# The experts' 512-column weight blocks laid out even columns first, and read by every product a column of either half in turn

## The chip, the cores and the metric

The kernel runs on one core of one Trainium2 chip. The metric is device time in microseconds, of the slowest (here the only) core. Before the change it is 1811.17 us, the median of three runs (1811.16 to 1812.86).

## The reference

A decoder trunk of two layers for 272 token rows (256 tokens and 16 learned meta rows), width 1024. Each layer is a token mixer (two linear-attention branches with their projections), a layer norm, a channel mixer and a second layer norm. The channel mixer of layer 0 is a dense SwiGLU; that of layer 1 is a top-2-of-8 expert SwiGLU with a hidden width of 3584. It is the experts that the change touches:

```
def swiglu(x, w_gate, w_up, w_down):
    return (jax.nn.silu(x @ w_gate) * (x @ w_up)) @ w_down

def moe_swiglu(x, w_router, w_gate, w_up, w_down):
    ...
    out = jnp.zeros(t.shape, jnp.float32)
    for e in range(N_EXPERTS):
        out = out + combine[:, e:e + 1] * swiglu(t, w_gate[e], w_up[e], w_down[e]).astype(jnp.float32)
```

All weights are float32: 8 x (1024 x 3584) for gate and for up, 8 x (3584 x 1024) for down, 352 MB in all.

## The kernel before

**Weights as units.** The host reorders the weights so that one load brings a unit: 128 partitions x 2048 float32 (1 MB), `UNIT`. SyncE loads the units in the order in which they are used into `raw`, a ring of six. ScalarE writes a rounded copy (`w_hi`, type float32r, a ring of three), VectorE writes the remainder raw - w_hi (`w_lo`, also float32r, a ring of three). A product of two float32 matrices is then three TensorE products, low x high, high x low, high x high (`mm3`, lines 796 to 800), accumulated in PSUM in float32.

**The experts' stage.** The tokens of an expert (up to 128) are gathered into `xg_hi`, `xg_lo`, transposed, so that they are the stationary operand (128 x 128); the weights are the moving operand, 512 columns at a time (`COLS`). An expert has seven chunks (`JCH`) of 512 hidden columns. A chunk is six units: two for gate, two for up (in each four blocks of 128 rows x 512 columns, `gate_or_up`, line 1153), two for down (in each two blocks of 128 rows x 1024 columns, read as two halves of 512, `down`, line 1186). That is 16 block products for gate and up and 8 for down, each of three matmuls: 72 matmuls of 512 columns in a chunk. Beside them stand four transposes of the gated hidden values (`turn_piece`, line 1176). Eight experts give 56 chunks. `expert` (from line 1233) orders them; on TensorE it is one straight line of work, with a wait on `lo_ready` before each unit (`expert_unit`, line 1149) and a signal `units_used` behind each.

**Who waits for whom.** ScalarE's rounding of a unit waits for the load of the unit and for `units_used` of the unit three before it. VectorE's remainder waits for ScalarE's `hi_ready` (`lo`, line 1999). SyncE's load into a slot of `raw` waits for `lo_ready` of the unit six before it. Between them VectorE also multiplies gate by up (line 2330) and makes the remainder of the turned hidden values (line 2320), ScalarE takes silu and rounds the hidden values.

**The rest of the kernel** (both token mixers, the dense SwiGLU, norms, router) has the weights as the stationary operand (128 x 128) and the tokens as the moving one, 272 or 256 columns (`feature_major`). Some of its products are in plain float32: attention (`inside`, line 999, whose moving operand is read in pieces of 32 columns, and `across`, line 1003, whose moving operand is one run of 256), the score products and the router.

Of the kernel before, what the change touches and what calls it, by code (L numbers as in the profile page):

```python
# [28 lines left out]
P = 128  # L29
D = 1024  # L30
# [10 lines left out]
EXPERTS = 8  # L41
# [4 lines left out]
COLS = 512  # L46
ROW = 320
RAW, HALVES = 6, 3
JCH = DFFE // COLS
# [58 lines left out]
def dense_units():  # L108

    stream = []  # L110

    def add_cols(src, c0, cols=COLS):
        for k in range(0, KT, 4):
            stream.append(("cols", src, k, 4, c0, cols))

    for l in range(DEPTH):
        w_in = ("w_in", l)
        def pair(src, c0):
            add_cols(src, c0)
            add_cols(src, c0 + COLS)  # L120

        if l == 0:
            stream.extend(("cols", w_in, k, 1, COL["gk"], COLS) for k in range(4))
            stream.extend(("cols", w_in, k, 2, COL["gk"], COLS) for k in (4, 6))
        else:
            add_cols(w_in, COL["gk"])
        add_cols(w_in, COL["gq"])
        stream.append(("twice", w_in, 0, KT, COL["ga"], P))
        pair(w_in, COL["gv"])
        add_cols(w_in, COL["gate_a"])  # L130
        add_cols(w_in, COL["gate_a"] + COLS)
        add_cols(w_in, COL["gate_b"])
        pair(w_in, COL["gr"])
        add_cols(w_in, COL["rq"])
        add_cols(w_in, COL["rk"])
        pair(w_in, COL["rv"])
        pair(("w_pa", l), 0)
        pair(w_in, COL["rg"])
        add_cols(w_in, COL["gate_b"] + COLS)
        pair(("w_pb", l), 0)  # L140
        pair(("w_o", l), 0)
        if l == 0:
            for c0 in range(0, DFF, COLS):
                n = min(COLS, DFF - c0)
                add_cols(("ffn_w_gate", 0), c0, n)
                add_cols(("ffn_w_up", 0), c0, n)
            for c in range(2):
                for k in range(0, DFF // P, 4):
                    stream.append(("cols", ("ffn_w_down", 0), k, min(4, DFF // P - k), c * COLS, COLS))
    return stream  # L150


def unit_major(a, rows):

    *lead, r, c = a.shape
    a = a.reshape(*lead, r // rows, rows // P, P, c).swapaxes(-3, -2)
    return a.reshape(*lead, r // rows, P, rows // P * c)


def weight_units(inputs):  # L160

    stream = dense_units()
    dense = np.zeros((len(stream), P, UNIT), np.float32)
    for u, (kind, (name, i), k, kn, c0, n) in enumerate(stream):
        cols = np.arange(c0, c0 + n) if kind == "cols" else c0 + np.arange(n) % RANK
        dense[u, :, 0:kn * n] = unit_major(np.asarray(inputs[name])[i][k * P:(k + kn) * P, cols], kn * P)[0]
    units = dict(dense_units=dense, moe_w_down=unit_major(np.asarray(inputs["moe_w_down"][0]), 2 * P))
    for name in ("moe_w_gate", "moe_w_up"):
        a = np.asarray(inputs[name][0]).reshape(EXPERTS, D, JCH, COLS).swapaxes(1, 2)
        units[name] = unit_major(a, 4 * P)  # L170
    return units

# [23 lines left out]
def trunk(nc, w, consts, where, out):  # L196

    ctx = ExitStack()
    with ctx:
# [43 lines left out]
        def quadrant(h, rows=BLOCK):  # L243
            return slice(h * BLOCK, h * BLOCK + rows)
# [299 lines left out]

        plan_sets()
        number = {(l, name): r for r, (l, name, _, _) in enumerate(sets)}
        ends = [u for _, _, u, _ in sets]
        NSETS = len(sets)

# [110 lines left out]
        block = ctx.enter_context(nc.Block())  # L660
# [131 lines left out]
        def _(pe):  # L792
            used = 0

            def mm3(dst, l_hi, l_lo, r_hi, r_lo, start, stop):


                nc.tensor.matmul(dst, l_lo, r_hi, start=start, stop=False)  # L798
                nc.tensor.matmul(dst, l_hi, r_lo, start=False, stop=False)  # L799
                return nc.tensor.matmul(dst, l_hi, r_hi, start=False, stop=stop)  # L800
# [85 lines left out]
            def repeated(columns, times):  # L886
                return columns.unsqueeze(1).broadcast_to([P, times, columns.shape[1]])
# [140 lines left out]
            for l in range(DEPTH):  # L1028
# [12 lines left out]
                for h in range(HEADS):  # L1041
                    last = nc.tensor.matmul(pt[:, h, 0:T], a2[quadrant(h), l, :], gaT[quadrant(h), :], start=True, stop=True)
# [79 lines left out]
            for t in range(2):  # L1122
                last = nc.tensor.transpose(pt[:, 2, (t + 1) * P:(t + 2) * P], mean_and_std[:, t, :], ident)
# [16 lines left out]
            last = nc.tensor.matmul(pt[0:1, 2, 0:P], ones[:, 0:1], repeated(sel[:, 1, :], P // EXPERTS), start=False, stop=True)  # L1140
# [5 lines left out]
            Y = ps[1][:, 0:2, :]  # L1146
            X = ps[1][:, 2:4, :]

            def expert_unit(at, u):
                pe.wait_ge(lo_ready, u + 1)  # L1150
                return w_hi[:, at % HALVES, :], w_lo[:, at % HALVES, :]

            def gate_or_up(dst, at, u, o, gathers_of=None, woven=None):
                for i in range(2):
                    if woven is not None and i == 1:
                        turn_may(woven)
                    if gathers_of is not None:
                        pe.wait_ge(gather_hi_ready, START + 4 * gathers_of + 2 * o + i + 1)
                        pe.wait_ge(gather_lo_ready, START + 4 * gathers_of + 2 * o + i + 1)
                    u_hi, u_lo = expert_unit(at + i, u + i)  # L1160
                    for k in range(4):
                        if woven is not None and i == 1:
                            turned = turn_piece(k)
                            if k == 3:
                                turned.then_inc(hidden_turned, 1)
                        last = mm3(dst, xg_hi[:, o, 4 * i + k, :], xg_lo[:, o, 4 * i + k, :],
                                   u_hi[:, k * COLS:(k + 1) * COLS], u_lo[:, k * COLS:(k + 1) * COLS],
                                   start=(i == 0 and k == 0), stop=(i == 1 and k == 3))
                    last.then_inc(units_used, 1)

            def turn_may(k):

                pe.wait_ge(hidden_ready, START + k + 1)
                pe.wait_ge(hidden_lo_ready, START + k)

            def turn_piece(i):
                return nc.tensor.transpose(TB[:, i * P:(i + 1) * P], a_sl[:, i * P:(i + 1) * P], ident)  # L1177

            def turn(k):

                turn_may(k)
                for i in range(4):
                    last = turn_piece(i)
                last.then_inc(hidden_turned, 1)

            def down(at, u, k, first, final, by_half=False, hidden=None, turns=False):
                a_hi, a_lo = hidden or (ag_hi, ag_lo)
                pe.wait_ge(hidden_lo_ready, START + k + 1)
                for i in range(2):
                    if i and turns:  # L1190
                        turn(k + 1)
                    u_hi, u_lo = expert_unit(at + i, u + i)
                    halves_last = by_half and i == 1
                    for a in range(2):
                        for b in range(2):
                            kk, q = (b, a) if halves_last else (a, b)
                            o = kk * D + q * COLS
                            last = nc.tensor.matmul(Y[:, q, :], a_lo[:, 2 * i + kk, :], u_hi[:, o:o + COLS],  # L1198
                                                    start=first and i == 0 and kk == 0, stop=False)
                            nc.tensor.matmul(Y[:, q, :], a_hi[:, 2 * i + kk, :], u_lo[:, o:o + COLS], start=False, stop=False)  # L1200
                            last = nc.tensor.matmul(Y[:, q, :], a_hi[:, 2 * i + kk, :], u_hi[:, o:o + COLS],  # L1201
                                                    start=False, stop=final and i == 1 and kk == 1)
                            if halves_last and (q, kk) == (0, 1):
                                last.then_inc(half_full, 1)
                    last.then_inc(units_used, 1)
# [27 lines left out]
            def expert(m, g, e, o, seam=False, more=False, closing=False, spilled=False):  # L1233
# [22 lines left out]
                if seam:  # L1256
                    chunk(0, final=True, moved=(o == 0), entry=True)
                else:
                    pe.wait_ge(silu_ready, START + k0)
                    gate_or_up(G_, at, u0, o, gathers_of=m)  # L1260
                    pe.wait_ge(hidden_ready, START + k0)
                    gate_or_up(U_, at + 2, u0 + 2, o)
# [1244 lines left out]
```

## Time and profile before

| | |
|---|---|
| median of three runs | 1811.17 us |
| the profiled execution, its own time | 1812.49 us |
| its span, first to last instruction | 1810.8 us |
| TensorE clock granted, mean | 0.998 of full |
| TensorE busy | 1778.4 us, 98% |
| VectorE busy | 1361.4 us, 75% |
| ScalarE busy | 1112.7 us, 61% |
| HBM read | 485.85 MB |

Busy times are from a hardware profile of one execution. Matmuls are pipelined: the duration shown for one (some 390 ns for 512 columns) is longer than the distance from its start to the next one's start, so what a matmul costs is read from starts, not from durations.

### The profile page before, as it was taken

How to read it: one execution, taken by the hardware profiler on the slowest of the kernel's cores; microseconds unless marked ns; L12 is line 12 of the kernel's file. 1: busy time of each engine (PE TensorE's matmuls, PEld its weight loads, DVE VectorE, ACT ScalarE, POOL GpSimd, SP SyncE). 2: the span in 40 equal slices, each digit the busy share in tenths (PEclk: the TensorE clock that was granted, in tenths of full speed). 3: DMA queues.
4: the chain of work that ended last, by engine and by line, in shares of the span. 5: the costliest groups of instructions: out<-in, count | busy, mean ns of one | idle time of the engine just before them, and what ended most of it. 6: DMA issues, size and time to landing. Idle time of an engine off the chain costs nothing.

```text
span 1810.8 us, 28116 instructions
## 1 busy us (share of the span) xinstructions
PE 1778.4 (98%) x10872; PEld 1579.2 (87%) x10872; DVE 1361.4 (75%) x1155; ACT 1112.7 (61%) x854; POOL 77.5 (4%) x145
## 2 busy tenths in 40 slices
PE   8999999999999999999999999999999999999997
PEld 7999999999989999998887888888888888888885
DVE  4756577645466566668888888888888888888897
ACT  5544254543445442557777777777777777777775
POOL 0300200000001102000000000000000000000200
PEclk9999999999999999999999999999999999999999
DMA  8635434444535465355999989999999999999993
GB/s 337 212 125 180 165 143 161 163 163 161 195 143 186 147 208 191 114 204 202 381 365 377 377 335 387 364 381 380 350 371 366 368 386 369 350 371 369 403 419 145
DMA packets 75922, 498.63 MB, mean 275 GB/s; under 512 B 11162, under 2 KB 11674, under 8 KB 17968
## 3 DMA queue, kind: packets, MB, share of 16 engines
q1 hardware_dynamic: 68304, 482.38, 69.9%
q0 software_dynamic: 5920, 11.58, 1.9%
q10 hardware_dynamic: 1600, 3.31, 0.7%
q8 instruction: 69, 1.13, 0.2%
q14 instruction: 29, 0.24, 0.0%
HBM read 485.85 MB, written 4.72 MB: 271 GB/s over the span
## 4 chain that ended last, share of the span: by engine, by line
PE 58%; DVE 1%; issue 0%; ACT 0%; DVEq 0%; ACTq 0%
PE ps L798 13%; PE ps L800 13%; PE ps L799 13%; PE ps L1198 6%; PE ps L1200 6%; PE ps L1201 6%; PE ps L1177 1%; PE ps L1221 1%; DVE w_lo L2003 0%; PE ps L895 0%; PE ps L999 0%; PE ps L1003 0%; DVE y_out L1946 0%; DVE h_tok L2402 0%; PE ps L989 0%
## 5 line engine op out<-in xcount | busy, mean ns | idle before, releaser
L2003 DVE TENSOR_TENSOR w_lo<-raw,w_hi 128x2048 fp32r<-128x2048 f32 x335 | 764.8, 2291 | 117.1 <-ACT w_hi L1327 114.4
L1327 ACT ACTIVATE w_hi<-raw 128x2048 fp32r<-128x2048 f32 x337 | 643.7, 1912 | 189.5 <-PE ps L800 103.0
L481 DVE TENSOR_TENSOR w_lo<-raw,w_hi 128x2048 fp32r<-128x2048 f32 (+2 forms) x126 | 272.5, 2170 | 192.5 <-ACT w_hi L470 191.7
L798 PE MATMUL ps<-rows_hi,w_lo 128*128 128x272 f32 (+1 forms) x1376 | 395.6, 287 | 13.0 <-DVE w_lo L481 8.1
L800 PE MATMUL ps<-rows_hi,w_hi 128*128 128x272 f32 (+1 forms) x1376 | 393.5, 286 | 0.0
L799 PE MATMUL ps<-rows_lo,w_hi 128*128 128x272 f32 (+1 forms) x1376 | 393.4, 286 | 0.0
L798 PE MATMUL ps<-w_hi,xg_lo 128*128 128x512 f32 x896 | 369.8, 413 | 0.0
L799 PE MATMUL ps<-w_lo,xg_hi 128*128 128x512 f32 x896 | 351.6, 392 | 0.0
L800 PE MATMUL ps<-w_hi,xg_hi 128*128 128x512 f32 x896 | 351.6, 392 | 0.0
L470 ACT ACTIVATE w_hi<-raw 128x2048 fp32r<-128x2048 f32 (+2 forms) x130 | 234.3, 1807 | 177.2 <-PE ps L800 139.0
L798 PEld LDWEIGHTS ps<-rows_hi,w_lo 128*128 128x128 f32 x1376 | 260.2, 189 | 15.6 <-DVE w_lo L481 8.1
L799 PEld LDWEIGHTS ps<-rows_lo,w_hi 128*128 128x128 f32 x1376 | 260.5, 189 | 0.1
L800 PEld LDWEIGHTS ps<-rows_hi,w_hi 128*128 128x128 f32 x1376 | 260.1, 189 | 0.0
L798 PEld LDWEIGHTS ps<-w_hi,xg_lo 128*128 128x128 f32 x896 | 168.5, 188 | 47.4
L800 PEld LDWEIGHTS ps<-w_hi,xg_hi 128*128 128x128 f32 x896 | 168.3, 188 | 38.1
L799 PEld LDWEIGHTS ps<-w_lo,xg_hi 128*128 128x128 f32 x896 | 169.2, 189 | 28.0
L1198 PE MATMUL ps<-w_hi,ag_lo 128*128 128x512 f32 x440 | 172.9, 393 | 0.5 <-DVE w_lo L2003 0.5
L1200 PE MATMUL ps<-w_lo,ag_hi 128*128 128x512 f32 x440 | 172.4, 392 | 0.0
L1201 PE MATMUL ps<-w_hi,ag_hi 128*128 128x512 f32 x440 | 172.1, 391 | 0.0
L1198 PEld LDWEIGHTS ps<-w_hi,ag_lo 128*128 128x128 f32 x440 | 82.7, 188 | 19.9 <-issue 1.6
L1201 PEld LDWEIGHTS ps<-w_hi,ag_hi 128*128 128x128 f32 x440 | 82.7, 188 | 18.3
L1200 PEld LDWEIGHTS ps<-w_lo,ag_hi 128*128 128x128 f32 x440 | 82.7, 188 | 17.5
(351 smaller groups left out, 1827.0 us busy)
## 6 DMA issues: line engine op xcount, KB each, us to landing
raw<-in_dense_units SPq DMA_DIRECT2D x116, 1024.0 KB, 4.9
raw<-in_moe_w_gate SPq DMA_DIRECT2D x112, 1024.0 KB, 7.0
raw<-in_moe_w_up SPq DMA_DIRECT2D x112, 1024.0 KB, 6.8
raw<-in_moe_w_down SPq DMA_DIRECT2D x112, 1024.0 KB, 7.2
raw<-in_dense_units SPq DMA_DIRECT2D x10, 512.0 KB, 3.8
result_rows<-rows POOLq DMA_DIRECT2D x7, 512.0 KB, 8.2
v_tok<-turned_v POOLq DMA_DIRECT2D x48, 64.0 KB, 2.9
srT<-o_tok ACTq DMA_DIRECT2D x6, 272.0 KB, 4.5
```

What stands on the lines that cost most here:

```text
L470: nc.scalar.activation(w_hi[:, u % HALVES, 0:k * n], raw[:, u % RAW, 0:k * n], ACT.Copy).then_inc(hi_ready, 1)
L481: nc.vector.tensor_tensor(w_lo[:, u % HALVES, 0:k * n], raw[:, u % RAW, 0:k * n], w_hi[:, u % HALVES, 0:k * n].bitcast(F32), ALU.subtract) ...
L798: nc.tensor.matmul(dst, l_lo, r_hi, start=start, stop=False)
L799: nc.tensor.matmul(dst, l_hi, r_lo, start=False, stop=False)
L800: return nc.tensor.matmul(dst, l_hi, r_hi, start=False, stop=stop)
L1177: return nc.tensor.transpose(TB[:, i * P:(i + 1) * P], a_sl[:, i * P:(i + 1) * P], ident)
L1198: last = nc.tensor.matmul(Y[:, q, :], a_lo[:, 2 * i + kk, :], u_hi[:, o:o + COLS], start=first and i == 0 and kk == 0, stop=False)
L1200: nc.tensor.matmul(Y[:, q, :], a_hi[:, 2 * i + kk, :], u_lo[:, o:o + COLS], start=False, stop=False)
L1201: last = nc.tensor.matmul(Y[:, q, :], a_hi[:, 2 * i + kk, :], u_hi[:, o:o + COLS], start=False, stop=final and i == 1 and kk == 1)
L1221: last = nc.tensor.matmul(ps[1 - half][:, 2 + k // 2, (k % 2) * 2 * P:(k % 2 + 1) * 2 * P], x_[:, t, f:f + P], S[:, t, :, :].rearrange("p ...
L1327: return nc.scalar.activation(dst, src, ACT.Copy, **kw)
L2003: tt(w_lo[:, at % HALVES, :], raw[:, at % RAW, :], w_hi[:, at % HALVES, :].bitcast(F32), ALU.subtract).then_inc(lo_ready, 1)
```

## The change

On the host the columns of the three expert weights are reordered inside each block of 512: the 256 even columns first, then the 256 odd ones. In the kernel the moving operand of every expert product is the same block, read through a view of two dimensions, 256 steps of one element around 2 steps of 256 elements: element 0, 256, 1, 257, ..., that is a column of either half in turn. The columns reach TensorE in their first order; the outputs, the order of the products, the loads, the rounding and all waits are as before.

```
+def evens_first(a):
+
+    *lead, c = a.shape
+    return a.reshape(*lead, c // COLS, COLS // 2, 2).swapaxes(-2, -1).reshape(*lead, c)
...
-    units = dict(dense_units=dense, moe_w_down=unit_major(np.asarray(inputs["moe_w_down"][0]), 2 * P))
+    units = dict(dense_units=dense, moe_w_down=unit_major(evens_first(np.asarray(inputs["moe_w_down"][0])), 2 * P))
     for name in ("moe_w_gate", "moe_w_up"):
-        a = np.asarray(inputs[name][0]).reshape(EXPERTS, D, JCH, COLS).swapaxes(1, 2)
+        a = evens_first(np.asarray(inputs[name][0])).reshape(EXPERTS, D, JCH, COLS).swapaxes(1, 2)
...
+            def in_turn(block):
+                return block.rearrange("p (b a) -> p a b", b=2)
...
                         last = mm3(dst, xg_hi[:, o, 4 * i + k, :], xg_lo[:, o, 4 * i + k, :],
-                                   u_hi[:, k * COLS:(k + 1) * COLS], u_lo[:, k * COLS:(k + 1) * COLS],
+                                   in_turn(u_hi[:, k * COLS:(k + 1) * COLS]), in_turn(u_lo[:, k * COLS:(k + 1) * COLS]),
                                    start=(i == 0 and k == 0), stop=(i == 1 and k == 3))
...
-                            last = nc.tensor.matmul(Y[:, q, :], a_lo[:, 2 * i + kk, :], u_hi[:, o:o + COLS],
+                            moving_hi, moving_lo = in_turn(u_hi[:, o:o + COLS]), in_turn(u_lo[:, o:o + COLS])
+                            last = nc.tensor.matmul(Y[:, q, :], a_lo[:, 2 * i + kk, :], moving_hi,
                                                     start=first and i == 0 and kk == 0, stop=False)
-                            nc.tensor.matmul(Y[:, q, :], a_hi[:, 2 * i + kk, :], u_lo[:, o:o + COLS], start=False, stop=False)
-                            last = nc.tensor.matmul(Y[:, q, :], a_hi[:, 2 * i + kk, :], u_hi[:, o:o + COLS],
+                            nc.tensor.matmul(Y[:, q, :], a_hi[:, 2 * i + kk, :], moving_lo, start=False, stop=False)
+                            last = nc.tensor.matmul(Y[:, q, :], a_hi[:, 2 * i + kk, :], moving_hi,
                                                     start=False, stop=final and i == 1 and kk == 1)
```

## Rows read from the trace of the kernel before

**Rows 1.** The page: the chain that ended last, by engine and line.
```profile
PE 58%; DVE 1%; issue 0%; ACT 0%; DVEq 0%; ACTq 0%
```

**Rows 2.** Stretches: us, busy (x instructions) of PE, PEld, DVE, ACT, POOL, clock, DMA share, GB/s.
```profile
850.00:1785.00 935.00, 934.50 (x4225) 760.05 (x4224) 821.36 (x485) 696.11 (x455) 14.01 (x13) 1.00 0.95 371
1000.00:1016.70 16.70, 16.70 (x77) 13.60 (x76) 14.58 (x9) 12.31 (x9) 0.00 (x0) 1.00 0.93 367
1780.00:1811.00 31.00, 18.41 (x80) 13.86 (x78) 22.09 (x31) 13.06 (x17) 0.00 (x0) 0.86 0.10 39
```

**Rows 3.** Waits inside the experts' stage (850 to 1785 us): total us, times, longest.
```profile
DVE w_lo L2003 <- ACT w_hi L1327: 112.0, 189, 3.1
ACT w_hi L1327 <- PE ps L800: 101.7, 153, 0.9
PE ps L1198 <- DVE w_lo L2003: 0.5, 1, 0.5
```

**Rows 4.** Groups of TensorE instructions by shape: count, busy us, mean ns, idle before.
```profile
L799 PE MATMUL ps<-w_lo,xg_hi 128*128 128x512 f32 x896 | 351.6, 392 | 0.0
L1200 PE MATMUL ps<-w_lo,ag_hi 128*128 128x512 f32 x440 | 172.4, 392 | 0.0
L1200 PE MATMUL ps<-w_lo,xg_hi 128*128 128x512 f32 x8 | 3.1, 392 | 0.0
```

**Rows 5.** TensorE timeline, experts' stage: start us, duration us; the 1st and 17th matmul.
```profile
1002.29 0.40 PE L798 MATMUL ps<-w_hi,xg_lo 128*128 128x512 f32 x1
...
1005.96 0.39 PE L799 MATMUL ps<-w_lo,xg_hi 128*128 128x512 f32 x1
```

**Rows 6.** TensorE timeline, token mixer, 272 moving columns; the 1st and 19th matmul.
```profile
259.76 0.28 PE L799 MATMUL ps<-rows_lo,w_hi 128*128 128x272 f32 x1
...
261.98 0.28 PE L799 MATMUL ps<-rows_lo,w_hi 128*128 128x272 f32 x1
```

**Rows 7.** TensorE timeline, attention in plain float32, 256 moving columns (x: matmuls together).
```profile
729.88 0.59 PE L999 MATMUL ps<-v_tok,o_tok 128*128 128x256 f32 x2
730.31 0.59 PE L1003 MATMUL ps<-srT,bT 128*128 128x256 f32 x2
730.74 1.03 PE L999 MATMUL ps<-v_tok,o_tok 128*128 128x256 f32 x4
731.60 1.03 PE L1003 MATMUL ps<-srT,bT 128*128 128x256 f32 x4
732.47 0.38 PE L999 MATMUL ps<-v_tok,o_tok 128*128 128x256 f32 x1
```

**Rows 8.** TensorE timeline, router in plain float32, 126 moving columns.
```profile
818.99 0.61 PE L895 MATMUL ps<-wr_g,hF 128*128 128x126 f32 x4
819.44 0.61 PE L1090 MATMUL ps<-tab,sgA 128*128 128x128 f32 x4
```

**Rows 9.** Groups of VectorE instructions by shape.
```profile
L2003 DVE TENSOR_TENSOR w_lo<-raw,w_hi 128x2048 fp32r<-128x2048 f32 x335 | 764.8, 2291 | 117.1 <-ACT w_hi L1327 114.4 <-DVE comb L2300 0.9 <-PE ps L1201 0.5
L481 DVE TENSOR_TENSOR w_lo<-raw,w_hi 128x1024 fp32r<-128x1024 f32 x8 | 9.7, 1224 | 14.5 <-ACT w_hi L470 14.5
L2320 DVE TENSOR_TENSOR ag_lo<-ps,ag_hi 128x512 fp32r<-128x512 f32 x55 | 37.6, 683 | 0.0
L1816 DVE TENSOR_REDUCE wr_sums<-wr_g 128x8 f32<-128x64 f32 x1 | 0.3, 269 | 0.0
L2432 DVE TENSOR_REDUCE row_f<-row_rank 128x4 f32<-128x32 f32 x1 | 0.2, 188 | 0.0
L2312 DVE TENSOR_REDUCE plan_f<-plan_f 1x1 f32<-1x8 f32 x3 | 0.4, 149 | 0.1
```

**Rows 10.** The page, DMA issues: KB each, us from issue to landing.
```profile
raw<-in_moe_w_gate SPq DMA_DIRECT2D x112, 1024.0 KB, 7.0
raw<-in_moe_w_up SPq DMA_DIRECT2D x112, 1024.0 KB, 6.8
raw<-in_moe_w_down SPq DMA_DIRECT2D x112, 1024.0 KB, 7.2
```

## The prediction

> **What bounds the kernel now.** I read the chain of waits first: of what ended last, TensorE holds 58% and no other engine more than 1% [rows 1]; the chain's remainder is not put down to an engine. So I checked the busy time of the stage that the change touches. From 850 to 1785 us TensorE is busy 934.50 of 935.00 us at a granted clock of 1.00 [rows 2]. VectorE is busy 821.36 us there, 88%, ScalarE 696.11 us, 74%, and the DMA engines 95%. All of them are close behind TensorE, but TensorE waits for none of them: in the whole stage its only wait for a remainder is 0.5 us, while ScalarE waits 101.7 us for TensorE to release a ring slot and VectorE 112.0 us for ScalarE [rows 3]. TensorE paces the stage, with the others held back by the rings. Whatever a matmul of 512 columns costs more or less is therefore paid in full, until another engine is the slower one.
>
> What one costs is the distance between starts. From the first to the seventeenth of a run of them it is 1005.96 - 1002.29 = 3.67 us for 16, or 229.4 ns [rows 5]. At 272 columns it is 2.22 us for 18, or 123.3 ns [rows 6]. The difference, 106.1 ns for 240 columns, is 0.442 ns a column, and what is left over is 3 ns. So the time of a matmul here is nearly all streaming of the moving operand, at 2.26 columns a ns, a little under one column a cycle at 2.4 GHz (0.417 ns). That is what the change can touch: it alters the order in which the moving operand is read from SBUF, and nothing else. One chunk confirms the sum: 72 x 229.4 ns = 16.5 us, and a stretch of 16.70 us holds 77 matmul records, one over the 76 (72 and four transposes) of a chunk [rows 2].
>
> **The change part by part.**
>
> The host's reordering of columns costs nothing on the device: the units have the same bytes and the same shape, so the 336 loads of 1024 KB stay as they are [rows 10].
>
> ScalarE's rounding and VectorE's remainder work on a whole unit element by element, in memory order; they don't see which column an element is. Neither instruction nor wait changes. No step is moved past another, no queue gets a new entry, and no wait is added or taken away.
>
> The matmuls change: 3 x (896 + 440 + 8) = 4032 of them [rows 4], which is 56 chunks of 72. Each now reads 512 elements of 4 bytes from two places 1024 bytes apart in turn, so that no two elements that follow each other are neighbours in memory. The stationary operand, its loads and the PSUM outputs are unchanged. The trace of before has no float32r moving operand read so. I bound its price from both sides.
>
> Lower end: a memory that hands over any element as readily as the next one costs nothing, 229.4 ns as now. Below nothing: the present 229.4 ns is 16.1 ns over 512 columns at one a cycle of 2.4 GHz (213.3 ns). If that surplus came from collisions in the present order and the new order avoided them all, 4032 x 16.1 ns = 65 us would be gained; the span would be 1746 us.
>
> Nearest rows for a less favourable read. In the attention products of layer 1, L999 takes its moving operand in runs of 32 columns and L1003 in one run of 256. Both come 0.43 us apart for two, 12 matmuls in 732.47 - 729.88 = 2.59 us, 216 ns each [rows 7]. Breaking the operand into runs of 32 is thus free, but both are plain float32, which streams slower whatever the order: 216 ns for 256 columns against 0.45 / 4 = 112.5 ns for 126 [rows 8] is 0.80 ns a column, little more than half the float32r rate. The one kind of read here that jumps at each element is VectorE's reduction over a stride of nine elements: 269 ns for 64 elements into 8, where the contiguous one takes 188 ns for 32 into 4 and 149 ns for 8 into 1 [rows 9]. From 8 to 32 contiguous elements it is 39 / 24 = 1.6 ns an element; from there to the 64 jumping ones 81 / 32 = 2.5 ns, a ratio of 1.56. Against the plain rate of VectorE, (2291 - 1224) / 1024 = 1.04 ns an element [rows 9], the jumping reduction has at most (269 - 149) / 56 = 2.14 ns, a ratio of 2.06. So there is a sign, on another engine and on one small instruction, that jumping at each element costs between 1.0 and 2.06 times. The upper end that I keep is wider: VectorE's element time of 2.14 ns, taken over as it is, would be 4.8 times TensorE's 0.442 ns; I return to that among the rivals.
>
> The value that I take is half rate, one column at 1.2 GHz. It is the rate at which the plain float32 products stream in this trace (0.80 ns, nearest to 0.83), that is a rate that TensorE's input has shown beside the full one, and it is near the upper ratio of VectorE's. A matmul then takes 512 x 0.833 = 427 ns and the some 10 ns that are over at 272 columns (123.3 against 113.3 ns at 2.4 GHz [rows 6]): 437 ns, 207 ns more than now. For 4032 that is 836 us. Nothing covers it, as TensorE has no idle time in the stage. What stands beside it gets slack instead: a chunk would last 16.7 + 72 x 0.207 = 31.6 us, with VectorE's 14.58 us in it [rows 2], and the DMA share would fall from 0.95 to about 0.5. The last 31 us of the span, layer norm and output [rows 2], are only shifted. The sum is 1810.8 + 836 = 2647 us for the span. The profiled execution took 1812.49 us in its own time, 1.3 us above the median of the three runs; against the median, 1811.17 + 836 gives 2647 us as well.
>
> The Trainium skill, page "Advanced Engine Details and Errata", section "SBUF Cachelines", says that SBUF is read in lines of 16 bytes, that at least two accesses in a row must hit a line to hide the memory's latency, and that a new line at each access is slower. By that rule the change is the bad case exactly, four hits a line becoming one; it gives no factor, and nothing in the trace of before tests it on TensorE. The page "TensorE: Matmul & The Clock Gate" of the Trainium skill, section "Step-by-step: what each phase is for", says that one column enters each cycle, so that throughput is purely the number of columns; by that alone the sum would be zero and the time that of before, 1811 us. The present slope of 0.442 ns a column is 6% above the 0.417 ns of such a rule.
>
> **The rivals.**
>
> *The order doesn't matter (no change, 1811 us).* TensorE's input may take elements from memory faster than it streams them, or keep a line of either half at hand, since each half for itself is read in sequence. For it: runs of 32 were free [rows 7]. Against it: those were at half the column rate, with 31 of 32 steps still to the neighbour, and VectorE's reduction shows a surcharge. Price 0, time 1811 us. This is the case on the other side: it decides if two interleaved sequential streams are served at 2.26 columns a ns.
>
> *The memory's line time is longer than a cycle of 1.2 GHz (4 times, about 4370 us).* If each new place costs two such cycles, 1.67 ns, a matmul takes 853 + 10 = 863 ns, 634 more, and 4032 of them 2556 us. For it: VectorE's jumping read at up to 2.14 ns an element, which would give 1096 ns a matmul and some 3494 us more, 5305 us. Against it: the contiguous reduction already has 1.6 ns an element, so most of the 2.14 is the reduction itself, and 2.5 against 1.6 is a much smaller ratio than four.
>
> *A partial price (1.1 to 1.7 times).* By the ratio 1.56 a matmul would take 229.4 x 1.56 = 358 ns, 128 more, in all 518 us, 2329 us. Below it lies the case in which TensorE reads at full rate, but its many more accesses slow its neighbours: VectorE needs 14.58 of 16.70 us a chunk, so its 6 x 2.291 us of remainders [rows 9] could grow by 2.1 us, 15%, before it is the bound; beyond that each further per cent is 0.14 us x 56 = 8 us.
>
> *Faster*, by up to the 65 us above.
>
> **How the numbers follow.** Half rate 0.40; no change 0.30; partial 0.12; four times and beyond 0.15; faster 0.03. The likeliest is half rate, 2647 us; its own range is 2540 to 2720 us (0.80 ns a column, no surcharge, 410 ns a matmul, to exactly twice the present slope, 455 ns). As a quarter to a third of the chance lies at no change, the 8-in-10 range must reach there: 1808 to 2720 us holds 0.82 and leaves out faster and four times. About 0.2% (3.6 us) can be told from no change; faster by more 0.03, within 0.30, slower by more 0.67.
>
> **What would show it.** In the changed profile starts of neighbouring matmuls in the experts' stage should lie 437 ns apart at a granted clock of 1.00, those of 272 columns at 123 ns as before; the first 850 us should be the same to a microsecond; VectorE's share in the stage should fall from 88% to about 46% and ScalarE's wait for TensorE grow by some hundred us, with VectorE's mean of 2291 ns for a unit unchanged. The forecast is wrong if the distance stays at 229 ns, if it is near 860 ns, or if the distance stays and VectorE's 2291 ns grows.

## The result, and the profile after

The changed kernel takes 1761.11 us, the median of four runs (1760.09 to 1761.86), beside 1811.34 us for the kernel before: a ratio of 0.9722, 95% interval 0.971 to 0.9735. It is 50.2 us faster. The prediction said 2647 us, range 1808 to 2720 us, with a chance of 0.03 for faster.

First the stretches that answer to [rows 2]: us, then busy time of PE, PEld, DVE, ACT and POOL with their instructions, granted clock, DMA share, GB/s. The stage now ends some 50 us earlier.

```profile
850.00:1735.00 885.00, 881.52 (x4221) 762.83 (x4220) 815.69 (x479) 693.77 (x454) 12.66 (x13) 1.00 0.98 391
1000.00:1016.70 16.70, 16.70 (x81) 14.49 (x80) 15.49 (x10) 12.65 (x9) 0.00 (x0) 1.00 0.98 388
```

The same 16.70 us now hold 81 matmul records instead of 77. The distance between starts shows why. In the timeline of TensorE (start, duration), the rows that answer to [rows 5]:

```profile
1001.84 0.38 PE L1208 MATMUL ps<-w_hi,ag_lo 128*128 128x512 f32 x1
...
1005.51 0.38 PE L806 MATMUL ps<-w_hi,xg_hi 128*128 128x512 f32 x1
```

The second is the 17th after the first: 3.67 us / 17 = 215.9 ns. Before it was 229.4 ns [rows 5]. A matmul gained 13.5 ns, 4032 of them 54.4 us. It is now 512 columns at 2.4 GHz (213.3 ns) and 2.6 ns over. The clock was granted at 1.00 before and after.

The groups of instructions show that nothing else changed its own time (busy us, mean ns, then idle time before them):

```profile
L2013 DVE TENSOR_TENSOR w_lo<-raw,w_hi 128x2048 fp32r<-128x2048 f32 x335 | 760.3, 2289 | 72.3 <-ACT w_hi L1337 67.8
L805 PE MATMUL ps<-rows_lo,w_hi 128*128 128x272 f32 x1088 | 313.6, 288 | 0.0
L1210 PE MATMUL ps<-w_lo,ag_hi 128*128 128x512 f32 x440 | 166.8, 379 | 0.0
```

VectorE's remainder of a unit stays at 2289 ns against 2291 [rows 9], the dense part's 272-column matmul has a mean of 288 ns before and after, and only the 512-column ones went from 392 ns [rows 4] to 379. The waits inside the stage (total us, times, longest), against [rows 3]:

```profile
ACT w_hi L1337 <- PE ps L806: 75.8, 151, 0.7
DVE w_lo L2013 <- ACT w_hi L1337: 65.4, 137, 2.7
PE ps L1208 <- DVE w_lo L2013: 2.5, 5, 1.2
```

ScalarE waits less for TensorE than before (75.8 us against 101.7) and VectorE less for ScalarE (65.4 against 112.0), while TensorE waits a little more for VectorE: it is idle 885.00 - 881.52 = 3.5 us in the stage, where it was 0.5 us. That closes the sum: 54.4 - 3 = 51.4 us against 1810.8 - 1759.1 = 51.7 us of span.

### The profile page after: what moved, and what is told of

It reads as the page before. It is cut to its first block, busy times and chain, and to the rows that moved or that the text cites. A ratio compares the mean times of both kernels' runs of the same rounds, so it can differ in the third digit from the quotient of the medians.

```text
span 1759.1 us, 28116 instructions
## 1 busy us (share of the span) xinstructions
PE 1723.6 (98%) x10872; PEld 1581.7 (90%) x10872; DVE 1356.2 (77%) x1155; ACT 1110.9 (63%) x854; POOL 76.3 (4%) x145
## 4 chain that ended last, share of the span: by engine, by line
PE 52%; DVE 3%; ACT 1%; issue 1%; DMA 1%; ACTq 0%; DVEq 0%
PE ps L804 11%; PE ps L805 11%; PE ps L806 11%; PE ps L1208 6%; PE ps L1211 5%; PE ps L1210 5%; DVE w_lo L2013 2%; PE ps L1186 1%; ACT w_hi L1337 1%; PE ps L1231 1%; DMA raw<-in_moe_w_up 1%; DVE ag_lo L2330 0%; PE ps L901 0%; PE ps L1009 0%; PE ps L1005 0%
## 5 line engine op out<-in xcount | busy, mean ns | idle before, releaser
L2013 DVE TENSOR_TENSOR w_lo<-raw,w_hi 128x2048 fp32r<-128x2048 f32 x335 | 760.3, 2289 | 72.3 <-ACT w_hi L1337 67.8
L804 PE MATMUL ps<-w_hi,xg_lo 128*128 128x512 f32 x896 | 357.2, 399 | 0.4 <-DVE w_lo L2013 0.2
L805 PE MATMUL ps<-w_lo,xg_hi 128*128 128x512 f32 x896 | 339.6, 379 | 0.0
L806 PE MATMUL ps<-w_hi,xg_hi 128*128 128x512 f32 x896 | 339.6, 379 | 0.0
L1208 PE MATMUL ps<-w_hi,ag_lo 128*128 128x512 f32 x440 | 167.7, 381 | 3.0 <-DVE w_lo L2013 2.5
L1210 PE MATMUL ps<-w_lo,ag_hi 128*128 128x512 f32 x440 | 166.8, 379 | 0.0
L1211 PE MATMUL ps<-w_hi,ag_hi 128*128 128x512 f32 x440 | 166.8, 379 | 0.0
```

The costliest lines, as they stand in the source:

```text
L1210: nc.tensor.matmul(Y[:, q, :], a_hi[:, 2 * i + kk, :], moving_lo, start=False, stop=False)
L2013: tt(w_lo[:, at % HALVES, :], raw[:, at % RAW, :], w_hi[:, at % HALVES, :].bitcast(F32), ALU.subtract).then_inc(lo_ready, 1)
```

## The experiments

In all of them the question is one: why does a matmul that reads 4-byte columns from two places in turn run faster than one that reads neighbours, where a half rate was forecast?

**The read by itself.** A kernel of groups of 24 matmuls. All read their moving operand from one loaded tile, each group through another view of 512 columns; the stationary operand changes with every matmul, as in the real kernel. The views, written out:

```
+ m = mov[:, 0:512]                                        # contiguous
+ m.rearrange("p (b a) -> p a b", b=2)                     # halves in turn (b=4: quarters)
+ m.rearrange("p (b a c) -> p a b c", b=2, c=2)            # runs of 2 from either half (c=4, 16)
+ m.rearrange("p (a b) -> p b a", b=2)                     # every 2nd column (b=4, 16)
```

> A kernel of its own, with none of the reference's computation: groups of 24 float32r matmuls on one loaded 128 x 2048 tile, each group with another view of the moving operand. First all forms with nothing else running, then contiguous and in turn beside ScalarE and VectorE copies (one after another of 128x2048), then beside 1 MB loads alone, then beside all three. In the kernel before, 512 contiguous columns came 229.4 ns apart, in the changed one 215.9 ns in turn. Theory A (the stream itself): contiguous 4-byte columns lose time by themselves, some 6%, with the memory otherwise idle. Then the quiet groups show 229 ns contiguous and 216 ns in turn, the same beside all traffic; 272 contiguous columns 123 ns, in turn 116 ns. Theory B (collisions with the neighbours): quiet contiguous groups run at 216 ns like in turn, and 229 ns appears only beside the copies or only beside the loads. Of the other views: if what counts is that two reads that follow each other lie in different places of memory, four quarters in turn is 216 ns too, and runs of 2, 4, 16 columns from either half climb back from 216 to 229 ns; a step of 16 or 64 bytes inside the block (every 4th, every 16th column) would be 216 ns by theory A if only a re-read of one line costs, and 430 ns or more by the rule of 16-byte lines, which the change has already broken once. Runs of two written to PSUM as runs of two (both sides in turn): same as in turn if PSUM takes it, else some hundred ns more.

The timeline of TensorE in that kernel (start us, length of the group, x: matmuls in it); the distance from one group's start to the next one's, over 24, is the time of a matmul:

```profile
34.37 5.34 PE L123 MATMUL ps<-mov,still 128*128 128x512 f32 x24
39.55 6.96 PE L128 MATMUL ps<-mov,still 128*128 128x512 f32 x24
46.34 8.16 PE L133 MATMUL ps<-mov,still 128*128 128x512 f32 x24
54.33 6.17 PE L138 MATMUL ps<-mov,still 128*128 128x512 f32 x24
60.34 5.92 PE L143 MATMUL ps<-mov,still 128*128 128x512 f32 x24
66.09 10.99 PE L148 MATMUL ps<-mov,still 128*128 128x512 f32 x24
76.91 11.22 PE L153 MATMUL ps<-mov,still 128*128 128x512 f32 x24
87.95 10.58 PE L158 MATMUL ps<-mov,still 128*128 128x512 f32 x24
98.35 3.19 PE L163 MATMUL ps<-mov,still 128*128 128x272 f32 x24
101.38 2.94 PE L168 MATMUL ps<-mov,still 128*128 128x272 f32 x24
104.16 4.36 PE L173 MATMUL ps<-mov,still 128*128 128x272 f32 x24
...
185.65 5.34 PE L123 MATMUL ps<-mov,still 128*128 128x512 f32 x24
190.83 5.62 PE L118 MATMUL ps<-mov,still 128*128 128x512 f32 x24
196.29 5.34 PE L123 MATMUL ps<-mov,still 128*128 128x512 f32 x24
```

L123 is halves in turn: 5.18 us, 216 ns. Then quarters 283 ns, runs of two 333, of four 250, of sixteen 240; every 2nd, 4th and 16th column 451, 460 and 433. The idea that successive reads only have to lie in different places missed: it expected 216 for the quarters and at most 229 for the runs. Further, 272 columns contiguous (L163) 126 ns, in turn (L168) 116. L118 is contiguous: 5.46 us, 227.5 ns. The granted clock was 1.00 in all these groups. The last three rows are beside traffic; the stretches for it (columns as above):

```profile
116.00:143.00 27.00, 27.00 (x122) 22.73 (x121) 20.91 (x10) 20.99 (x12) 0.00 (x0) 1.00 0.00 1
169.50:201.50 32.00, 32.00 (x146) 27.17 (x146) 15.65 (x8) 15.65 (x9) 0.00 (x0) 1.00 1.01 421
```

In the first VectorE and ScalarE copy without DMA, in the second 421 GB/s of loads run, and copies beside them for half of the time. The 216 and 228 ns are the same in both. Theory B, collisions with the other engines and the loads, is refuted. Theory A holds in the main: with all of them at rest a contiguous read of 512 float32r columns takes 11.7 ns (5%) longer than one in turn. The forecast's price is there too, 451 ns, but for a step, not for two places in turn.

Two things stay open. The kernel gained 13.5 ns a matmul, and its contiguous read took 229.4 ns where the groups have 227.5 with or without traffic; where those 1.9 ns come from no run shows. And TensorE's own weight loads ran beside every group (PEld busy 22.73 of 27.00 us in the first stretch), so no run tells a loss of the stream alone from a loss of the stream beside the weight load.

**Gate and up alone.** The change undone for the down weights:

```
-                            moving_hi, moving_lo = in_turn(u_hi[:, o:o + COLS]), in_turn(u_lo[:, o:o + COLS])
+                            moving_hi, moving_lo = u_hi[:, o:o + COLS], u_lo[:, o:o + COLS]
```

> The changed kernel with the down weights laid out and read as before; gate and up in turn. 2688 of the 4032 matmuls keep the saving of 13.5 ns, 1344 lose it. By theory A (each matmul saves for itself): 1811.2 - 36.3 = 1775 us, or 1761.1 + 18.1 = 1779 us counted from the changed kernel; L1208's matmuls again 229 ns apart, the others 216. By theory B with the relief coming from a whole stage in which fewer places collide, both kinds would move together. If the changed kernel is held back by VectorE and the loads, giving 1344 x 13.5 ns back costs less than 18 us: about 1765 to 1773 us.

Measured 1780.0 us (1779.28 to 1780.97; ratio to before 0.9824, 0.9808 to 0.984). That is the 1779 of theory A. The two kinds of matmul lie side by side in its timeline of TensorE:

```profile
1001.30 0.38 PE L804 MATMUL ps<-w_hi,xg_lo 128*128 128x512 f32 x1
...
1001.95 0.39 PE L1208 MATMUL ps<-w_hi,ag_lo 128*128 128x512 f32 x1
...
1006.08 0.39 PE L1208 MATMUL ps<-w_hi,ag_lo 128*128 128x512 f32 x1
```

The three in turn take 0.65 us, 217 ns each; the 18 contiguous ones behind them take 4.13 us, 229.4 ns each. So each matmul saves for itself.

**Which places.** A second kernel of groups:

> A kernel of its own, with none of the reference's computation: again groups of 24 matmuls with nothing else running. The first such kernel gave for 512 float32r columns: contiguous 228 ns, halves in turn 216, four quarters in turn 283, runs of two from either half 333, every 2nd or 4th column 451 and 460. Theory C (two readers): the even and the odd columns of the stream are fetched separately, each is fast while its next element lies in the 16 bytes it last fetched, and the two hinder each other a little in one place. It expects: halves 4096 bytes apart, or 257 elements apart, 216 ns; blocks of 4, 8, 16 or 64 columns read with a partner block in turn (elements 0, 4, 1, 5, ...) 216 to 220 ns; blocks of 2 (0, 2, 1, 3, 4, ...) 228 to 250; eight places in turn at least 283; each column twice (0, 0, 1, 1) about 228. Theory D (only distance counts: successive columns must lie far apart, by a multiple of 1024 bytes): 257 apart and blocks of 4 to 64 are no better than 228, and eight places in turn would be 216; four in turn at 283 already speaks against it. Plain float32, 256 columns: 216 ns contiguous and in turn, by theory C also with a step of 4, as its stream is half as fast; bfloat16 512 columns: 216 ns contiguous, no gain in turn, a loss for a step of 4 or 8.

Again starts of groups on TensorE; L114 is blocks of 2 (elements 0, 2, 1, 3), L119 blocks of 4 (0, 4, 1, 5), L139 contiguous from element 1, L144 each column twice, L149 eight places in turn. L174 and L179 are plain float32, contiguous and halves in turn, L194 is bfloat16 halves in turn; these three are taken up further below:

```profile
54.03 5.62 PE L114 MATMUL ps<-mov,still 128*128 128x512 f32 x24
59.49 5.34 PE L119 MATMUL ps<-mov,still 128*128 128x512 f32 x24
64.67 5.34 PE L124 MATMUL ps<-mov,still 128*128 128x512 f32 x24
...
80.21 5.86 PE L139 MATMUL ps<-mov,still 128*128 128x512 f32 x24
85.91 5.34 PE L144 MATMUL ps<-mov,still 128*128 128x512 f32 x24
91.08 11.89 PE L149 MATMUL ps<-mov,still 128*128 128x512 f32 x24
102.77 3.08 PE L164 MATMUL ps<-mov,still 128*128 128x256 f32 x24
...
108.37 10.53 PE L174 MATMUL ps<-src 128*128 128x256 f32 x48
118.73 13.28 PE L179 MATMUL ps<-src 128*128 128x256 f32 x48
...
158.68 11.79 PE L194 MATMUL ps<-mov,still 128*128 128x512 bf16 x24
```

Blocks of 2 take 227.5 ns, blocks of 4 take 215.8, as do blocks of 8, 16 and 64 and halves 257 or 1024 elements apart. So distance is not the cause (theory D falls). Eight places take 487 ns, the contiguous read from element 1 237.5. But each column twice takes 215.4 ns where theory C said 228. In theory C the even and the odd columns are two streams, fetched separately, that hinder each other in one place; here both are in the same 16 bytes, and nothing is lost. That led to theory E, which keeps the two streams and counts how many neighbours each takes from 16 bytes. A third kernel of groups tested it:

> A kernel of its own, with none of the reference's computation: groups of 24 matmuls of 512 columns, nothing else running. So far: contiguous 228 ns, halves in turn 216, blocks of 4 with their partner 216, blocks of 2 (0, 2, 1, 3) 228, each column twice 215. Theory E: the even and the odd columns are fetched as two streams, and the time goes by how many neighbours a stream takes from 16 bytes before it moves on: four are free, two cost 6%, one costs double. Theory C (the streams hinder each other when both are in the same 16 bytes) already fails on each column twice. Streams in different places, E: two of each four neighbours, near (0, 4, 1, 5, then 8, 12, 9, 13) or in far halves 228; every second element of far halves 228; every fourth 430 to 490; four near places in turn 283 as the quarters. C: 216 for the first three. Contiguous from element 1 was 237; from element 2, 4 and 8: E says 4 and 8 are 228, 2 is 228 too if each stream still takes two per 16 bytes. In turn from element 1 or 2: 216. bfloat16 (8 elements in 16 bytes), contiguous 216, in turn 485: if its elements come in pairs of 4 bytes, runs of 2 and 4 from either half in turn get back towards 216; if the rule were the same as for 4 bytes, it would have been 216 in turn. Each bfloat16 column twice: 216 or, if pairs matter, 485.

The first rows are two of each four neighbours from near places (L104), the same from far halves (L109), every 2nd element of far halves (L114), every 4th of far halves (L119):

```profile
42.96 5.69 PE L104 MATMUL ps<-mov,still 128*128 128x512 f32 x24
48.48 5.65 PE L109 MATMUL ps<-mov,still 128*128 128x512 f32 x24
53.97 5.60 PE L114 MATMUL ps<-mov,still 128*128 128x512 f32 x24
59.41 11.04 PE L119 MATMUL ps<-mov,still 128*128 128x512 f32 x24
70.27 5.36 PE L99 MATMUL ps<-mov,still 128*128 128x512 f32 x24
...
152.16 11.80 PE L174 MATMUL ps<-mov,still 128*128 128x512 bf16 x24
```

230, 229, 227 and 452 ns: theory E, and not 216 as theory C had it. Four near places in turn took 269 ns (283 expected), halves in turn that start at element 1 or 2 took 217 and 216 (216 expected). All float32r groups of 512 columns in the three kernels, at a granted clock of 1.00 (each kernel's opening groups and the second's closing one left out), by the number of neighbours that a stream takes from 16 bytes before it moves on:

| neighbours per 16 bytes | views | ns a matmul of 512 |
|---|---|---|
| 4 | halves in turn, blocks of 4 to 64, each column twice | 215 to 217 |
| 2 | contiguous, blocks of 2, two of four, every 2nd of far halves | 227 to 238 |
| 2, but jumping between halves | runs of 4, runs of 16 | 250, 240 |
| 1, coming back to the same 16 bytes | quarters, four near places, runs of 2 | 283, 269, 333 |
| 1 | every 2nd, 4th, 16th column, every 4th of far halves | 433 to 460 |
| 1, coming back, of eight places | eight places in turn | 487 |

Theory E parts the groups at 216 ns from those near 228 and those over 430. It doesn't give the sizes between: where a stream jumps or comes back (250 to 333 ns, and 487 for eight places) the count alone orders nothing. It also missed for contiguous reads from element 2, 4 or 8, which take 232 to 234 ns where it said 228. And it doesn't carry to bfloat16: L174 is bfloat16 halves in turn, and its starts inside the group lie 484 ns apart, as those of L194 in the second kernel do (the granted clock 1.00 in both), where theory E would have eight neighbours a stream and no loss. By the same measure, starts inside the group, bfloat16 takes 216 ns contiguously, with each column twice and in runs of eight, 227 ns in runs of four and 271 ns in runs of two.

**Quarters in the kernel.** `b=4` instead of `b=2` in the view and in the host's layout:

> The changed kernel with four quarters of each block in turn instead of two halves, laid out on the host to match; results as in the reference. If the matmul's own read sets the time, as in the kernel of groups, a matmul takes 283 ns instead of 216: 4032 x 67 = 270 us more than the changed kernel, 1761 + 270 = 2031 us. By a theory that spreading reads over more places relieves the memory it would be 1761 or less.

Measured 2007.5 us, one run, 246 us more than the changed kernel. Starts on TensorE:

```profile
1001.67 0.45 PE L1208 MATMUL ps<-w_hi,ag_lo 128*128 128x512 f32 x1
...
1003.35 0.45 PE L1208 MATMUL ps<-w_hi,ag_lo 128*128 128x512 f32 x1
```

1.68 us for six, 280 ns. The forecast of 2031 us was 24 us too high; 280 ns in place of 283 makes 12 of them, the rest isn't broken down. Spreading reads over more places is no relief in itself.

**Blocks of 4 in the kernel, and every 2nd column.** Layout and view:

```
+    return a.reshape(*lead, c // 8, 4, 2).swapaxes(-2, -1).reshape(*lead, c)
+                return block.rearrange("p (x b a) -> p x a b", b=2, a=4)
```

> The changed kernel with another layout of the experts' blocks: inside each 8 columns the four even ones first, and each product reads a column of either four in turn (elements 0, 4, 1, 5, ..., 8, 12, ...); results as in the reference. Theory E (what counts is that the even and the odd columns of the stream each take four neighbours from 16 bytes) expects what halves in turn gave, 216 ns a matmul and 1761 us. A theory by which the two places must lie far apart in memory expects 1811 us, as contiguous.

Measured 1760.55 us (1760.12 to 1761.41; ratio to before 0.9721, 0.9705 to 0.9737), the changed kernel's time. Two places 16 bytes apart do what two places 1024 bytes apart do.

```
+    return a.reshape(*lead, c // COLS, 2, COLS // 2).swapaxes(-2, -1).reshape(*lead, c)
+                return block.rearrange("p (a b) -> p b a", b=2)
```

> The changed kernel with a layout that makes each product read every second column of a block, then the other half of them (elements 0, 2, 4, ..., 1, 3, 5, ...); results as in the reference. Each of the two streams then steps by 16 bytes, one element from each 16. By theory E and the kernel of groups a matmul takes 451 ns instead of 216: 4032 x 235 = 948 us more than the changed kernel, 2709 us, near what the prediction gave to the change itself. VectorE and the loads have slack, so nothing else adds.

Measured 2712.3 us, one run, against 2709 expected. Its starts and one stretch (columns as above):

```profile
1001.59 0.65 PE L804 MATMUL ps<-w_hi,xg_lo 128*128 128x512 f32 x1
...
1008.85 0.65 PE L1210 MATMUL ps<-w_lo,ag_hi 128*128 128x512 f32 x1
850.00:2600.00 1750.00, 1750.00 (x4091) 811.71 (x4090) 811.59 (x471) 671.84 (x441) 10.37 (x13) 1.00 0.54 193
```

7.26 us for 16, 454 ns. VectorE's share is down to 46% and the DMA share to 0.54. This is the picture that the prediction drew, in another change than the one at hand.

**The tokens too.** In the dense parts the moving operand is the tokens, written by ScalarE and VectorE. The same trick there needs alternating writes:

```
-                copy(hT_hi[0][:, 2 * i:2 * i + 2, :], hF[:, 2 * i:2 * i + 2, :]).then_inc(columns_hi_ready, 1)
+                copy(by_halves(hT_hi[0][:, 2 * i:2 * i + 2, :]), in_pairs(hF[:, 2 * i:2 * i + 2, :])).then_inc(columns_hi_ready, 1)
...
-                                   rowtile(x_hi_, k0 + k)[:, cols], rowtile(x_lo_, k0 + k)[:, cols],
+                                   by_halves(rowtile(x_hi_, k0 + k), cols), by_halves(rowtile(x_lo_, k0 + k), cols),
```

> The changed kernel, and in the dense parts too (both token mixers, dense SwiGLU) the moving operand, the tokens' rounded and remainder copies, is stored by ScalarE and VectorE even tokens first and read by halves in turn; results as in the reference. Theory A (each contiguous float32r read loses some 6% by itself): 5808 matmuls of 272 or 256 columns go from 123.3 ns to 116 ns, 7 ns each, 41 us less where TensorE is the bound: 1761 - 41 = 1720 us, and 1725 to 1735 if the writers of the copies get slower or other engines become the bound in places. If their alternating writes cost ScalarE or VectorE twice their time, some 60 instructions of about 0.7 to 1.3 us each become that much longer, of which perhaps a third stands on the path: 1735 to 1745 us. A theory by which the gain belongs to the experts' stage alone (weights just written, 1 MB loads beside) expects 1761 or more.

Measured 1735.23 us (1733.58 to 1736.83; ratio to before 0.9578, 0.9562 to 0.9594), 25.9 us below the changed kernel. A matmul of 272 columns gained what was expected:

```profile
259.08 0.28 PE L815 MATMUL ps<-zT_lo,w_hi 128*128 128x272 f32 x1
...
261.17 0.28 PE L815 MATMUL ps<-zT_lo,w_hi 128*128 128x272 f32 x1
```

The second is the 18th after the first, 2.09 us / 18 = 116 ns, where it was 123.3 [rows 6]. Part of the 41 us expected from this is given back by the writers. Groups of VectorE and ScalarE, then waits of TensorE:

```profile
L2236 DVE TENSOR_TENSOR aT_lo<-aT_f,aT_hi 128x1088 fp32r<-128x1088 f32 x5 | 10.9, 2190 | 11.4 <-ACT aT_hi L1347 11.4
L1347 ACT ACTIVATE aT_hi<-aT_f 128x1088 fp32r<-128x1088 f32 x5 | 10.8, 2157 | 25.7 <-DVE aT_f L2233 25.7
```

```profile
PE ps L814 <- DVE rows_lo L1939: 6.0, 4, 2.0
PE ps L814 <- DVE zT_lo L2222: 3.7, 2, 1.9
```

In the changed kernel the same two take 1292 and 1115 ns. Compared with the instructions of 544 elements (1164 and 1180 ns now, 725 and 659 before), an element takes 1.89 ns instead of 1.04 on VectorE and 1.80 instead of 0.84 on ScalarE. ScalarE only writes in turn; VectorE also reads the rounded copy in turn, so its figure is not one of the write alone. TensorE waits 6.0 us for the rows (3.3 us in the changed kernel) and 3.7 us for the merged operand, which it did not wait for at all: 6.4 of the 15 us that are missing. So that operand was made contiguous again:

```
+                    split = not name.startswith("wo")
-                copy(by_halves(m_hi[c], width(l)), in_pairs(sgA[:, 4 * c:4 * c + 4, width(l)])).then_inc(act_done, 1)
+                copy(m_hi[c][:, :, width(l)], sgA[:, 4 * c:4 * c + 4, width(l)]).then_inc(act_done, 1)
```

> The kernel with tokens in turn too (1735 us), but with the merged operand of the w_o products (192 matmuls) stored and read contiguously again; results as in the reference. Those matmuls lose 192 x 7 ns = 1.3 us; the four writers of each of rounded and remainder copy, that TensorE waits for, take 1.1 and 1.2 us instead of 2.1 each, and the wait of 3.7 us before those products goes. If the slow alternating writes on the path are what kept the token version from its 1720 us, this is 1731 to 1734 us; if they stood beside other work, 1736.

Measured 1732.24 us (1731.96 to 1733.24; ratio to before 0.9561, 0.9545 to 0.9577), the fastest version here. And with only the normed rows in turn:

> Of the token version only the normed rows (1376 x 3 matmuls) are stored and read by halves in turn, the gated rows, the merged operand and the dense SwiGLU's hidden rows are contiguous again; results as in the reference. 1680 matmuls lose 7 ns, 12 us; their writers get back 0.5 us (16 + 16 of them) and 1.0 us (12 of ScalarE and VectorE each), up to 30 us of engine time, of which I expect a third on the path. So 1735 to 1740 us: each matmul saves for itself, and a write in turn only costs where TensorE waits for it. If it is below 1731, most of the writers' loss was on the path.

Measured 1737.85 us (1737.24 to 1738.66; ratio to before 0.9589, 0.9573 to 0.9605). So of the writes in turn, those of the merged operand (192 matmuls) cost 3.0 us more than they brought, and those of the gated and the hidden rows (1488 matmuls) brought 5.6 us. Whether the number of matmuls decides this, or how closely TensorE waits for the writer, these runs don't separate.

## Why the prediction was wrong

What bounds the kernel was read rightly: TensorE paces the experts' stage, and what a 512-column matmul gains or loses is paid in full. The count of 4032 matmuls and the untouched time of a load, a copy and a remainder held, the first 850 us too (TensorE busy 830.40 us there, 830.48 before), and the slack of the others nearly (3.5 us of waits).

The step that failed is the value taken for a matmul, "half rate, one column at 1.2 GHz", 437 ns, and with it the surcharge of 207 ns on each of 4032 matmuls, 836 us; a matmul measured 215.9 ns, 13.5 ns less than before. A price of that size exists, but for a different view. The prediction treated "no two elements that follow each other are neighbours" as the bad case. The float32r groups fit a picture in which the column after next counts: with halves in turn each second column is a neighbour, and four of them come from 16 bytes. Every 2nd column in sequence, which looks milder, is the view that costs 454 ns and gave 2712 us. That this lies near the forecast's 2647 is no support for its reasoning, which came from other engines and other types. The rule of the Trainium skill ("Advanced Engine Details and Errata", "SBUF Cachelines"), that accesses in a row must hit a line of 16 bytes at least twice, fits the float32r groups only if it is read for even and odd columns apart. There one hit is slow (433 to 460 ns in sequence) and two are nearly enough: by measurement they still take 227 to 238 ns where four take 215 to 217.

The second failing step is the lower end. The row was seen, 0.442 ns a column against 0.417 at 2.4 GHz, and the surplus of 16.1 ns was priced (65 us, of which 54 came). But it was put down to collisions and given 0.03. The rows of before could not have settled this: 512 columns have 16.1 ns over and 272 have 10 [rows 5, 6], but in stages with a DMA share of 0.95 [rows 2] and, over the first 850 us, 0.50, so the growth could belong to the columns or to the traffic. In the kernel of groups, without traffic, contiguous reads have 14.2 ns over at 512 columns and 12.9 at 272, and reads in turn 2.5 at both: there the loss hardly grows with the columns. What settled the question was measuring the read alone, in two orders.

The anchor for half rate was also misread. The plain float32 rows 216 ns apart [rows 7] were taken as matmuls. In the second kernel of groups 24 plain float32 matmuls leave 48 records (L174), 216 ns apart, so a matmul of 256 columns takes 431 ns in two records. What a record does in 216 ns, a slower read or more than one run through the columns, no run shows; so these rows were no evidence for the rate at which another view of float32r is read. The pieces in which L999 reads are also 64 columns long and not 32 (line 599 of the kernel before: `n = VRUN // HEADS`, 256 / 4). The reduction of VectorE with a jumping read was evidence for VectorE alone; in the token version reads and writes in turn about double the time of an element on VectorE and ScalarE (1.8 and 2.1 times), while the same alternation sped TensorE's read up.

## What to carry to other kernels

In this kernel a matmul with a contiguous float32r moving operand took 6% longer (229.4 against 215.9 ns at 512 columns, 123.3 against 116 at 272) than one laid out so that even and odd columns each run through four neighbours (halves, or blocks of four, in turn). The layout is free where the host makes it. For data written on the chip it has to be tried operand by operand, as an element written in turn took 2.1 times as long on ScalarE. Don't read with a step in sequence (433 to 460 ns) or from four places in turn (269 to 283), and don't carry the trick to bfloat16 or plain float32. When a measured time lies a few per cent over the engine's own rate, measure the instruction alone, in its order and in another, before setting the chance that the surplus can go.

## What the hardware showed that was not expected

Plain float32 (256 columns, two records of 216 ns each) goes the other way: halves in turn 273 ns a record and every 4th column 451, where theory C expected 216 for both. For bfloat16 halves in turn is 484 ns against 216. Writing PSUM in runs of two beside a read in runs of two took 333 ns, no more than the read alone. Why two neighbours from 16 bytes cost some 5% and four nothing, why a contiguous read from element 1 takes 237.5 ns, and why bfloat16 follows another rule stays open; the two streams are a model that fits the float32r groups, and no run looked into the engine.
